# Last expert of an encoder's MoE layer: result weighted ahead of its scatter, by column halves, and the stored results read back in four steps

## What is computed

```python
def moe_swiglu(h, w_router, b_router, w_gate, w_up, w_down):
    top_v, top_i = lax.top_k(logits, TOP_K)              # 2 of 8 experts for each token
    top_w = jax.nn.softmax(top_v, axis=-1)
    combine = jnp.sum(one_hot(top_i, 8) * top_w[..., None], axis=-2)
    for e in range(N_EXPERTS):
        out = out + combine[..., e:e + 1] * swiglu(h, w_gate[e], w_up[e], w_down[e])
...
x = x + g2[:, None, :] * moe_swiglu(...)
return modulate(rmsnorm(x, final_norm_g), fsh, fsc)
```

## Time and profile before

| what | value |
|---|---|
| median of 3 runs | 1620.88 us (1620.31 to 1623.54) |
| the profiled execution's own time | 1624.67 us |
| its span in the trace | 1622.6 us |
| PE busy | 1541.9 us (95%) |
| DVE busy | 1335.0 us (82%) |
| ACT busy | 983.9 us (61%) |
| POOL busy | 198.5 us (12%) |
| DMA, mean over the span | 313 GB/s |

### The profile page before, as it was taken

One profiled execution on the slowest core, in us unless ns is written; L12 is line 12 of the kernel. 1 busy time (PEld: TensorE's weight loads), 2 busy tenths in 40 slices (PEclk: granted clock), 3 DMA queues, 4 the chain that ended last, 5 costly groups with the idle time before them and its releaser, 6 DMA issues.

```text
span 1622.6 us, 20495 instructions
## 1 busy us (share of the span) xinstructions
PE 1541.9 (95%) x6814; PEld 1233.4 (76%) x6814; DVE 1335.0 (82%) x1062; ACT 983.9 (61%) x801; POOL 198.5 (12%) x188
## 2 busy tenths in 40 slices
PE   6999779899997899999999999999999999999996
PEld 6777547677776678777888888888888888888784
DVE  6799478877778758998888888888888888888897
ACT  4544523434435645676777777777777777777673
POOL 0499500000002002000000000000000000000600
PEclk9999989999998899999999999999999999999998
DMA  9899219698894247999999999999999999999992
GB/s 343 321 342 357 92 51 378 215 304 272 289 328 149 79 155 271 389 353 355 385 367 355 382 368 356 381 369 356 380 368 354 376 373 354 383 367 356 387 366 113
DMA packets 238894, 508.67 MB, mean 313 GB/s; under 512 B 15494, under 2 KB 38150, under 8 KB 238728
## 3 DMA queue, kind: packets, MB, share of 16 engines
q1 hardware_dynamic: 233824, 491.52, 83.8%
q0 software_dynamic: 4448, 14.55, 2.5%
q10 hardware_dynamic: 584, 2.11, 0.3%
HBM read 502.12 MB, written 7.87 MB: 314 GB/s over the span
## 4 chain that ended last, share of the span: by engine, by line
PE 84%; DVE 9%; issue 2%; DMA 2%; ACT 2%; SPq 0%; DVEq 0%; ACTq 0%
PE bank L1798 26%; PE bank L1799 26%; PE bank L1800 26%; PE bank L2146 2%; DVE lo L1547 1%; PE bank L1779 1%; DMA stage<-in_l_moe_w_up 1%; PE bank L1895 1%; DVE hs L1211 1%; DVE lo L1131 1%; DVE lo L1445 1%; DMA stage<-in_l_moe_w_gate 1%; PE bank L2025 0%; DVE hs L1169 0%; PE bank L1793 0%
## 5 line engine op out<-in xcount | busy, mean ns | idle before, releaser
L1547 DVE TENSOR_TENSOR lo<-stage,hi 128x2048 fp32r<-128x2048 f32 x168 | 385.5, 2304 | 46.2 <-ACT hi L992 46.0
L992 ACT CAST hi<-stage 128x2048 fp32r<-128x2048 f32 x168 | 321.3, 1914 | 112.6 <-DMA stage<-in_l_moe_w_up 92.2
L1799 PE MATMUL bank<-lo,hg_hi 128*128 128x512 f32 x896 | 353.3, 394 | 0.0
L700 ACT CAST hi<-stage 128x2048 fp32r<-128x2048 f32 x71 | 135.5, 1911 | 146.6 <-PE bank L1800 72.4
L1799 PEld LDWEIGHTS bank<-lo,hg_hi 128*128 128x128 f32 x896 | 168.5, 188 | 37.2
L1131 DVE TENSOR_TENSOR lo<-stage,hi 128x2048 fp32r<-128x2048 f32 x71 | 163.8, 2311 | 31.5 <-ACT hi L700 25.5
L1547 DVE TENSOR_TENSOR lo<-stage,hi_h 128x2048 fp32r<-128x2048 f32 x56 | 128.3, 2291 | 63.7 <-ACT hi_h L992 63.7
L1798 PE MATMUL bank<-hi,hg_hi 128*128 128x512 f32 x452 | 178.6, 395 | 1.4 <-DVE lo L1547 1.2
L1800 PE MATMUL bank<-hi,hg_lo 128*128 128x512 f32 x452 | 178.8, 395 | 0.0
L1799 PE MATMUL bank<-lo,eaT_hi 128*128 128x512 f32 x448 | 177.2, 395 | 0.0
L1798 PE MATMUL bank<-hi,hT_hi 128*128 128x512 f32 x416 | 171.6, 413 | 4.1 <-DVE hT_lo L1239 2.3
(11 more groups left out here) (328 smaller groups left out, 2779.7 us busy)
## 6 DMA issues: line engine op xcount, KB each, us to landing
stage<-in_l_moe_w_gate SPq DMA_DIRECT2D x224, 512.0 KB, 4.9
stage<-in_l_moe_w_up SPq DMA_DIRECT2D x224, 512.0 KB, 5.2
stage<-in_l_moe_w_down SPq DMA_DIRECT2D x224, 512.0 KB, 4.9
ada_w<-in_l_ada_w SPq DMA_DIRECT2D x40, 1024.0 KB, 5.3
stage<-in_l_ret_w_in SPq DMA_DIRECT2D x48, 512.0 KB, 7.3
stage<-in_l_ffn_w_gate SPq DMA_DIRECT2D x22, 512.0 KB, 7.8
stage<-in_l_ffn_w_up SPq DMA_DIRECT2D x22, 512.0 KB, 8.7
stage<-in_l_ffn_w_down SPq DMA_DIRECT2D x22, 512.0 KB, 6.8
```

Source lines behind the costliest of these rows:

```text
L700: nc.scalar.copy(hi[:, b % HRING, :], stage[:, b % RING, :]).then_inc(hi_done, 1)
L992: nc.scalar.copy(hi_e(b), stage[:, b % RING, :]).then_inc(hi_done, 1)
L1547: nc.vector.tensor_tensor(lo[:, b % RING, :], stage[:, b % RING, :], hi_e(b).bitcast(F32), ALU.subtract).then_inc(lo_done, 1)
L1799: mm(dst_ap, a_hi, w_lo, start=False, stop=False)
```

## The change

Four things.

1. POOL issues the four reads of `y_dram` one at a time, each when PE has used a certain unit of the last pass (`U_END - 36`, `- 30`, `- 24`, `- 18`, six units apart), and does a token tile's sum when that tile's two reads have landed.
2. The last pass's down product for its last two units (`e_down_last`) is ordered by column half, so that the left half (bank 4) is finished twelve matmuls ahead of the right half (bank 5).
3. Each half is weighted ahead of the scatter: DVE multiplies it by a per-slot weight `ix[:, 30:31]` and by the gate `m` (`weigh_down`), ACT casts it, DVE subtracts, PE scatters, and DVE then only adds the scattered block to `xs` (`add_down`, four of 512 columns). The per-slot weights come from two float32 matmuls of one column on PE in `turn_pick`, two one-column copies and a register load on DVE ahead of it, and a one-column copy on ACT.
4. The register load of `last` no longer stands between the sums and the last products on DVE.

```diff
@@ POOL
             pool.wait_ge(scale_done, 5)
+            m = pool.value_load(meta[0:1, 2 * N_TAB + 1:2 * N_TAB + 2], min_val=0, max_val=3) * UNITS_ITEM
             for t in range(TT):
-                pool.dma_start(moe[:, t, :], yv[0, :, t, :]).then_inc(y_in, 16)
-                pool.dma_start(ysec[t][:, :], yv[1, :, t, :]).then_inc(y_in, 16)
-            pool.wait_ge(y_in, 64)
-            for t in range(TT):
+                for r, dst_ap in enumerate((moe[:, t, :], ysec[t][:, :])):
+                    pool.wait_ge(w_used, m + (RING + U_END - 36 + 6 * (2 * t + r)))
+                    pool.sem_inc(y_go, 1)
+                    pool.dma_start(dst_ap, yv[r, :, t, :]).then_inc(y_in, 16)
+                pool.wait_ge(y_in, 32 * t + 32)
                 nc.gpsimd.tensor_scalar(moe[:, t, :], moe[:, t, :], rsm[:, t, 5, 2:3], None, ALU.mult)
@@ ACT
+            def take_down(n):
+                act.wait_ge(dn_w, n + 1)
+                cols = slice(n * CB, (n + 1) * CB)
+                nc.scalar.copy(dn_hi[:, cols], dnw[n][:, :]).then_inc(dn_hi_done, 1)
...
             act.wait_ge(put_tr, extra + (E + 1))
+            nc.scalar.copy(ix[:, 30:31], bank[:, 3, SEQ:SEQ + 1])
             nc.scalar.copy(put[:, 0:SEQ], bank[:, 3, 0:SEQ]).then_inc(put_done, 1)
...
-            take_down(extra + E, m + (RING + U_END))
-            norm(4, (14, 16))
+            take_down(0)
+            take_down(1)
+            norm(4, (15, 16))
@@ DVE
+            def weigh_down(n):
+                dve.wait_ge(dn_part, n + 1)
+                cols = slice(n * CB, (n + 1) * CB)
+                nc.vector.scalar_tensor_tensor(out=dnw[n][:, :], in0=bank[:, 4 + n, :], scalar=ix[:, 30:31],
+                                               in1=mods[:, 1, 2, cols], op0=ALU.mult, op1=ALU.mult).then_inc(dn_w, 1)
+            def low_down(n):
+                dve.wait_ge(dn_hi_done, n + 1)
+                cols = slice(n * CB, (n + 1) * CB)
+                nc.vector.tensor_tensor(dn_lo[:, cols], dnw[n][:, :], dn_hi[:, cols].bitcast(F32),
+                                        ALU.subtract).then_inc(dn_done, 1)
...
             dve.wait_ge(put_tr, passes)
+            last = dve.value_load(meta[0:1, bass.ds(passes - 1, 1)], min_val=0, max_val=E - 1)
+            for t in range(TT):
+                nc.vector.tensor_copy(tokv[:, t, 9:10], comb[:, t, bass.ds(last, 1)])
             choose(pick, bass.ds(col, 1)).then_inc(pick_done, 1)
...
-                if t == TT - 1:
-                    low_down()
                 link(nc.vector.tensor_tensor(xs[:, t, :], xs[:, t, :], moe[:, t, :], ALU.add))
...
+            def add_down(i):
+                n, t = i // 2, i % 2
+                cols = slice(n * CB, (n + 1) * CB)
+                dve.wait_ge(scat, i + 1)
+                nc.vector.tensor_tensor(xs[:, t, cols], xs[:, t, cols], bank[:, (6, 4)[t] + n, :], ALU.add).then_inc(resid, 1)
+            weigh_down(0)
+            low_down(0)
+            weigh_down(1)
+            add_down(0)
+            low_down(1)
+            for i in range(1, 4):
+                add_down(i)
+            norm(4, (15, 16))
@@ PE
                 for t in range(TT):
-                    ins = nc.tensor.transpose(bank[:, 3, t * P:(t + 1) * P], pick[:, t, :].bitcast(F32), ident)
+                    nc.tensor.transpose(bank[:, 3, t * P:(t + 1) * P], pick[:, t, :].bitcast(F32), ident)
+                for t in range(TT):
+                    ins = mm(bank[:, 3, SEQ:SEQ + 1], pick[:, t, :].bitcast(F32), tokv[:, t, 9:10], start=(t == 0), stop=(t == TT - 1))
+            def e_down_last(b, more, n):
+                pe.wait_ge(e_lo, n + 1)
+                parts = [unit_e(b + g, 2, more) for g in range(2)]
+                for c2 in range(2):
+                    cols = slice(c2 * CB, (c2 + 1) * CB)
+                    for k in range(4):
+                        h, l = parts[k // 2]
+                        ins = three(bank[:, 4 + c2, :], eaT2_hi[:, k, :], eaT2_lo[:, k, :], h[:, k % 2, cols], l[:, k % 2, cols],
+                                    False, k == 3)
+                    ins.then_inc(dn_part, 1)
             def scatter():
-                pe.wait_ge(dn_done, 1)
                 pe.wait_ge(put_done, extra + (E + 1))
-                for t in range(TT):
-                    for n in range(2):
-                        cols = slice(n * CB, (n + 1) * CB)
+                for n in range(2):
+                    pe.wait_ge(dn_done, n + 1)
+                    cols = slice(n * CB, (n + 1) * CB)
+                    for t in range(TT):
                         mm(bank[:, (6, 4)[t] + n, :], put[:, t * P:(t + 1) * P], dn_hi[:, cols], start=True, stop=False)
-                        ins = mm(bank[:, (6, 4)[t] + n, :], put[:, t * P:(t + 1) * P], dn_lo[:, cols], start=False, stop=True)
-                    ins.then_inc(scat, 1)
+                        mm(bank[:, (6, 4)[t] + n, :], put[:, t * P:(t + 1) * P], dn_lo[:, cols], start=False, stop=True).then_inc(scat, 1)
```

More of the change, by code:

```diff
@@ L240, in encoder @@
         dn_lo = at("dn_lo", [D], R + 46 * KW, F32R)
+        dnw = [at("dnw0", [CB], R + 34 * KW), at("dnw1", [CB], R + 36 * KW)]
         wr = at("wr", [KT, E], R + 60 * KW + 128)
@@ L388, in encoder @@
         dn_out = sem("dn_out")
+        dn_part = sem("dn_part")
+        dn_w = sem("dn_w")
         snext_done = sem("snext_done")
@@ L1036, in e_high_act @@
                 nc.scalar.copy(dst[:, :, :], bank[:, 2, :].rearrange("p (k n) -> p k n", k=4)).then_inc(e_hi, 1)
-            def take_down(n, used):
-                act.wait_ge(w_used, used)
-                nc.scalar.copy(dn_hi[:, :], bank[:, 4:6, :].rearrange("p b n -> p (b n)")).then_inc(dn_hi_done, 1)
+            def take_down(n):
+                act.wait_ge(dn_w, n + 1)
+                cols = slice(n * CB, (n + 1) * CB)
+                nc.scalar.copy(dn_hi[:, cols], dnw[n][:, :]).then_inc(dn_hi_done, 1)
             def take_out(w, used):
@@ L1755, in _ @@
                 link(ins)
-                if t == TT - 1:
-                    low_down()
                 link(nc.vector.tensor_tensor(xs[:, t, :], xs[:, t, :], moe[:, t, :], ALU.add))
-            last = dve.value_load(meta[0:1, bass.ds(passes - 1, 1)], min_val=0, max_val=E - 1)
-            for t in range(TT):
[L1762 to L1768, removed]
+            dve.wait_ge(put_done, extra + (E + 1))
+            def add_down(i):
[11 more added lines that the diff above has]
+            norm(4, (15, 16))
         @block.tensor
@@ L2248, in _ @@
             e_down_step(U_END - 4, m, o + (E * N_EC - 2), False, False, between=o + (E * N_EC - 1))
-            e_down_step(U_END - 2, m, o + (E * N_EC - 1), False, True, eaT2_hi, eaT2_lo)
+            e_down_last(U_END - 2, m, o + (E * N_EC - 1))
             scatter()
```

## The result

Twenty runs of the changed kernel have a median of 1616.28 us, twenty of the kernel before 1626.38. The ratio is 0.9945 with a 95% interval of 0.9930 to 0.9959, so the change saves 0.55%, 8.9 us (6.7 to 11.4). Forecast were 7.8 us, from 1620.9 to 1613.1. The direction and the size of the change hold. The level doesn't: the three runs of before that were at hand (1620.31 to 1623.54) lie in the lower half of what the same kernel takes in more runs, 1619.2 to 1629.9. The plain median, 1616.28, lies inside the range, 1610.6 to 1617.2, but the ratio applied to the twenty runs of before gives 0.9945 x 1626.38 = 1617.4, just above its end. (One run of each kernel took over 3900 us; the ratio and the ranges given here leave both out.)

The account below looks back on a forecast made before the run. PE, busy 95% of the span, was taken as the bound, leaving its stalls and the tail to win. Terms -3.5 + 0.4 - 4.7 = -7.8 us took 1620.9 to 1613.1 us; range 1610.6 to 1617.2.

Parts of the forecast that it names:

- The bound and the two places: PE busy 95%; winnable were its 3.8 us loss behind the stored results' reads and the 9.4 us before the final norm.
- Part 1: Reads in steps in the last pass: the 3.8 us stall shrinks to 0.3, a gain of 3.5 us.
- Part 2: Two one-column float32 matmuls added on PE's path in the last pass: cost 0.4 us, bounds 0.2 and 0.5.
- Part 3: Tail by column halves: the final norm starts at 1609.45 in place of 1614.14, gain 4.7 us, bounds 3.5 and 5.2.
- rival A: Reads cost as much spread as together, so only the tail is won: 1616.6 us; chance 0.13.
- B: Each of POOL's three operations per tile stops DVE wholly, 2.5 us of stall per tile: 1617.8 us; chance 0.05.
- C: Tail gives half, as handoffs are in series and the left half starts late: gain 2.4 us, 1615.4 us; chance 0.10.
- D: Each of the four reads starves PE by itself, 15.2 us in place of 3.8: 1628.0 us; chance 0.03.

Follow-up runs that it names:

- reads_only: Kernel before with only POOL's four reads in steps, old tail; ratio 0.9965, S1 (seventh result's write to PE's last weight matmul) 106.93 us, S2 9.61 us.
- tail_only: Changed kernel with POOL's reads issued at once as before; ratio 0.9972, S1 110.29 us, S2 (PE's last weight matmul to final norm's first scaling) 4.47 us.
- attention_busy: Changed kernel with unused small matmuls where PE waits in layer 1's attention and ahead of the router; ratio 0.9970, S1 107.43 us, S2 4.76 us.
- nosum_before: Kernel before without POOL's weighting and adding of the stored results; S1 107.66 us, S2 9.77 us, no ratio timed.
- nosum_after: Changed kernel without POOL's weighting and adding of the stored results; S1 106.65 us, S2 4.54 us, no ratio timed.

## Why the prediction was right, and where it was wrong

**The bound and the two places**: right. PE was to be saved its 3.8 us stall and the tail to be shortened, and both happened.

**Part 1** (-3.5): the windows gave -3.55, and PE stood still for 0.05 us in them. The two causes, late weights and slowed DVE, are borne out: some 1.8 and 2.0 us, from one trace each. But the hole behind the windows belongs to this part too, since reads_only has it: by S1 the reads in steps gave -2.8. What I missed is a third thing that a late DVE does: the product `eact` comes late too, and a register load on PE shows as 0.7 us, where gaps under 0.5 us in sum were forecast. I had looked only at the lead of weights.

**Part 2** (+0.4, bounds 0.2 and 0.5): right. The matmuls took 0.34 us in the chain and lengthened PE's step by 0.45 in tail_only and 0.5 in the changed kernel. The other 0.7 us at that place is the hole of part 1.

**Part 3** (-4.7): -4.5 in the changed kernel's trace, -5.0 in tail_only. The difference of 0.5 has two halves: the scatter started 0.65 us after PE's last weight matmul and not 0.42 as in tail_only (forecast were 0.2), since DVE came to the tail late, and its last two matmuls were slow. attention_busy shows the first half alone (0.69 us, full rate, S2 4.76). The prices held within 0.1 us; furthest off were the half-width weighting (0.75, not 0.68) and ACT's cast (0.62, not 0.58). ACT stayed hidden.

**The sum**: -6.7 us in the trace where -7.8 were forecast; by the ratio -8.9, whose interval holds both.

**The level and the range** are where the prediction failed. It took 1620.9 us, the median of three runs, for the level of before, where twenty runs gave 1626.38; and it left "1.5 us for the scatter of the runs" at the low end and none at the high end, which is rival A and half a us. The same kernel scatters over 10 us. In the traces most of that arises long before the change and goes with the clock that PE is granted between 540 and 640 us: up to 1.7 us in the attention, up to 6 in the router. The single profiled execution, 3.8 us above the median shown, was the hint: the term should have been a scatter of 4 to 5 us to either side. By the same cause 2.7 us of the 9.4 between the two profiled spans are no gain of the change: the two stretches took 48.3 us in the changed kernel's trace and 51.7 in that of before.

**Rivals.** A (reads as dear as together): no, reads_only saved 2.8 us in S1. B (POOL locks DVE out in all three operations): no; leaving all of them out saved 0.83 us, forecast were 5.0. For DVE, the Trainium skill's rule (SBUF — State Buffer, "Who interferes with whom") that the second comer fully blocks fits the tensor_tensor alone: in the changed kernel the two subtractions beside it took 2.2 and 2.1 us longer than 2.29, those beside the tensor_scalars at most 0.5. There it was POOL's operation that took longer, 4.06 us where the earlier trace rows has 2.87. The reading against B in the prediction, 29.48 to 32.10 with "most of it in the one stretched subtraction", was too low, since one window holds 17 instructions of DVE and the other 16. One by one, five subtractions of the kernel before were stretched, by 5.2 us in sum, 2.2 and 1.6 of it beside the two tensor_tensors; in nosum_before none is. C (half the tail): no. D (each read starves PE): no at six units; at three units PE lost 2 us more than at six, but through DVE.

## What to carry to other kernels

Look up how much the runs of one kernel differ, and where in the trace that difference arises, before you put a range on a change of half a per cent; cut two traces at a common mark and compare the parts, not the spans.

A background operation is priced by what stands behind the instruction that it stretches: against nosum_after (six units apart, no sums) the same work cost 0.8 us of S1 six units apart, 1.9 five and 2.9 three units apart, in one trace each.

If the operand of an engine's next instruction comes just in time, a register load behind it can show up on the path (0.7 us here); put it ahead of the loop.

## What the runs showed of the hardware that I had not expected

PE's clock fell in the tail of the changed kernel: the granted clock was 1.00 up to 1602.4 and 0.71 in the next 1.7 us, 2.6 us after PE's last weight matmul, and the last two scatter matmuls took 0.58 and 0.63 us, not 0.39. In the other traces with the new tail all eight scatter matmuls ran at the full rate (0.39 to 0.50 us). The old tail differs in the same way. In the kernel before the scatter was over when the clock fell (1.00 until 1611.6). In reads_only, with the same tail and the same wait of 2.5 us ahead of the scatter, all eight matmuls took 0.62 to 0.63 us, at a clock (the third number from the end) that went from 0.92 to 0.50, half of full speed:

```profile
1599.40:1601.40 2.00, 0.55 (x2) 0.46 (x3) 1.91 (x2) 1.49 (x2) 0.00 (x0) 0.92 0.00 0
1601.40:1603.40 2.00, 2.00 (x7) 1.52 (x5) 0.96 (x2) 0.00 (x0) 0.00 (x0) 0.50 0.00 0
```

In nosum_before they took 0.52 to 0.79 us. S2 was 9.61 and 9.77 in these two, 9.43 in the kernel before. So a few tenths of a us in S2 can be the clock of that run and not the kernel's doing.

The time of one piece of code moved in steps with the clock: the router's stretch took 39.0, 40.7 or 45.0 us, with nothing between in the eleven traces that share its code.
